# The state-space recurrence of an encoder layer: a predicated copy in place of mask products, and another order of a chunk's work on five engines

## The reference

```python
lower = idx[:, None] >= idx[None, :]
seg = a_cs[..., :, None] - a_cs[..., None, :]
decay = jnp.exp(jnp.where(lower, seg, -jnp.inf))
cb = jnp.einsum('bclgn,bcsgn->bgcls', cc, bc)
y_diag = jnp.einsum('bgcls,bgkcls,bcsgkp->bclgkp', cb, decay, xdt)
...
y = y_fwd + y_bwd + xs * d_skip.reshape(g, kh)[..., None]
y = (y.reshape(b, l, D_SSD) * jax.nn.silu(z)).astype(z.dtype)
```

## Time and profile before

| | us |
|---|---|
| median of 3 runs | 2933.29 |
| lowest, highest | 2931.94, 2934.85 |
| profiled execution, span | 2933.2 |
| PE busy | 2833.0 (97%) |
| DVE busy | 1997.4 (68%) |
| ACT busy | 1312.2 (45%) |
| POOL busy | 594.4 (20%) |

### The profile page before, as it was taken

One profiled execution on the slowest core, in us unless ns is written; L12 is line 12 of the kernel. 1 busy time (PEld: TensorE's weight loads), 2 busy tenths in 40 slices (PEclk: granted clock), 3 DMA queues, 4 the chain that ended last, 5 costly groups with the idle time before them and its releaser, 6 DMA issues.

```text
span 2933.2 us, 36790 instructions
## 1 busy us (share of the span) xinstructions
PE 2833.0 (97%) x12912; PEld 2244.0 (77%) x12912; DVE 1997.4 (68%) x3119; ACT 1312.2 (45%) x2578; POOL 594.4 (20%) x818
## 2 busy tenths in 40 slices
PE   7999999999999999999999999999999999999996
PEld 5878787667777878888778787876677788888885
DVE  3657755774788887775647567457757877777656
ACT  4224555455743333345543255553557433333443
POOL 4622222450014530000100222235400000000001
PEclk9999999999999999999999999999999999999998
DMA  7551232204535541243522422331246222214334
GB/s 223 140 147 56 63 106 91 95 27 154 181 129 191 177 164 58 87 155 114 201 94 74 125 63 73 117 130 28 68 141 199 79 80 76 68 58 156 96 115 140
DMA packets 143575, 332.75 MB, mean 113 GB/s; under 512 B 17745, under 2 KB 18417, under 8 KB 143392
## 3 DMA queue, kind: packets, MB, share of 16 engines
q1 hardware_dynamic: 106032, 200.42, 21.7%
q0 software_dynamic: 37360, 129.97, 13.4%
HBM read 264.49 MB, written 67.80 MB: 113 GB/s over the span
## 4 chain that ended last, share of the span: by engine, by line
PE 76%; DVE 11%; issue 5%; POOL 4%; ACT 3%; DMA 1%; SPq 0%; DVEq 0%; ACTq 0%; POOLq 0%
PE A L1076 4%; PE A L1078 4%; PE A L1077 4%; PE G L1076 4%; PE G L638 4%; PE G L1078 4%; PE G L1077 4%; PE G L640 4%; PE G L639 4%; PE A L1128 4%; PE A L1130 4%; PE A L1129 4%; PE G L668 3%; PE G L669 2%; PE G L670 2%
## 5 line engine op out<-in xcount | busy, mean ns | idle before, releaser
L1715 DVE TENSOR_TENSOR wlo<-raw,whi 128x512 fp32r<-128x512 f32 x630 | 437.3, 700 | 483.0 <-ACT whi L1204 480.9
L1204 ACT CAST whi<-raw 128x512 fp32r<-128x512 f32 x630 | 383.2, 619 | 448.6 <-PE A L1130 150.8
L638 PE MATMUL G<-arena_rounded,whi 128*128 128x512 f32 x800 | 330.6, 413 | 7.0 <-DVE wlo L1715 4.2
L640 PE MATMUL G<-arena_rounded,wlo 128*128 128x512 f32 x800 | 316.3, 395 | 0.0
L639 PE MATMUL G<-arena_rounded,whi 128*128 128x512 f32 x800 | 316.2, 395 | 0.0
L1076 PE MATMUL A<-arena_rounded,whi 128*128 128x512 f32 x560 | 222.0, 396 | 1.5 <-DVE wlo L1715 1.0
L1076 PE MATMUL G<-arena_rounded,whi 128*128 128x512 f32 x560 | 221.9, 396 | 0.8 <-DVE wlo L1715 0.7
L1078 PE MATMUL A<-arena_rounded,wlo 128*128 128x512 f32 x560 | 221.5, 396 | 0.0
L1078 PE MATMUL G<-arena_rounded,wlo 128*128 128x512 f32 x560 | 221.5, 395 | 0.0
L1077 PE MATMUL G<-arena_rounded,whi 128*128 128x512 f32 x560 | 221.5, 395 | 0.0
L1077 PE MATMUL A<-arena_rounded,whi 128*128 128x512 f32 x560 | 221.4, 395 | 0.0
(11 more groups left out here) (356 smaller groups left out, 6257.2 us busy)
## 6 DMA issues: line engine op xcount, KB each, us to landing
raw<-w_gu_tiles SPq DMA_DIRECT2D x184, 256.0 KB, 3.3
raw<-w_out_rows SPq DMA_DIRECT2D x144, 256.0 KB, 2.8
raw<-w_tok_tiles SPq DMA_DIRECT2D x96, 256.0 KB, 2.7
raw<-w_in_tiles SPq DMA_DIRECT2D x92, 256.0 KB, 2.8
raw<-sums_of_down SPq DMA_DIRECT2D x88, 256.0 KB, 2.6
raw<-w_down_rows SPq DMA_DIRECT2D x66, 256.0 KB, 2.7
f_by_chunk<-small POOLq DMA_DIRECT2D x24, 512.0 KB, 4.6
arena<-w_down_rows POOLq DMA_DIRECT2D x22, 512.0 KB, 7.4
```

What stands on the lines that cost most here:

```text
L638: nc.tensor.matmul(out, whi[:, u % SPLIT_SLOTS, w], hi, start=first, stop=False)
L640: return nc.tensor.matmul(out, wlo[:, u % SPLIT_SLOTS, w], hi, start=False, stop=last)
L1204: nc.scalar.copy(whi[:, u % SPLIT_SLOTS, w], weights_of(u)).then_inc(S["hi_split"], 1)
L1715: tt(wlo[:, u % SPLIT_SLOTS, w], weights_of(u), whi[:, u % SPLIT_SLOTS, w].bitcast(F), ALU.subtract).then_inc(S["lo_split"], 1)
```

## The change

The mask products go. PE's `exponents` has 4 matmuls per call instead of 8, and one semaphore at its end. A new DVE operation `pick(c, g)` copies the backward differences over the forward ones where the source token is later (`copy_predicated`, mask tile in SBUF, data and target in PSUM). ACT then takes a single exp into SBUF, and DVE multiplies that by `cb`, both from SBUF. The diagonal of the backward pass, which the copy leaves out, moves into the skip factor: `cb`'s diagonal is needed per token, so SP writes `rows` to DRAM and reads the diagonal back (256 elements of 4 bytes), and POOL makes a coefficient with two small operations (128x16) ahead of the wide one.

```diff
-    nc.tensor.matmul(to[:, n, :], ident_r[:, :], mask[:, :].unsqueeze(1).broadcast_to([P, 4, P]), start=True, stop=False)
-    m = nc.tensor.matmul(to[:, n, :], tmp_r[:, less:less + P], tmp_r[:, rhs:rhs + HALF], start=False, stop=True)
+    m = nc.tensor.matmul(to[:, n, :], tmp_r[:, less:less + P], tmp_r[:, rhs:rhs + HALF], start=True, stop=True)
...
+def pick(c, g):
+    dve.wait_ge(S["eb_done"], nth("eb_done", 2 * c + g + 1))
+    nc.vector.copy_predicated(by_heads(spans(ef_pair(c))), later[...].broadcast_to([P, GH, P]),
+                              by_heads(spans(eb_pair(c)))).then_inc(S["picked"], 1)
 def masses(c, g):
-    dve.wait_ge(S["eb_exp"], nth("eb_exp", 2 * c + g + 1))
-    after(tt(e, e, t(2 * g), ALU.add))
-    tt(t(2 * g + 1), e, cb(c, g), ALU.mult)
+    tt(t(2 * g + 1), t(2 * g), cb(c, g), ALU.mult)
...
-def gated(c):
-    after(tt(y_, y_, yb(c), ALU.add))
-    tt(arena[:, ZT + c, :], y_, arena[:, ZT + c, :], ALU.mult).then_inc(S["u_ready"], 1)
+def with_within(c):
+    tt(yb(c), spans(p2), yb(c), ALU.add).then_inc(S["y_read"], 1)
+def times_gate(c):
+    dve.wait_ge(S["y_read"], nth("y_read", c + 1))
+    tt(arena[:, ZT + c, :], yb(c), arena[:, ZT + c, :], ALU.mult).then_inc(S["u_ready"], 1)
```

The orders of a middle chunk after:

```diff
+PE:   incoming(c,SB) [waits for decays(c,1)], incoming(c,SF), exponents(c+1,0), within(c,0),
+      inner(c+1), exponents(c+1,1), state(c), within(c,1)
+DVE:  from_behind(c), from_ahead(c), pick(c+1,0), masses(c,1), times_gate(c-1), pick(c+1,1),
+      next_state(c), masses(c+1,0), with_within(c)
+POOL: add(from behind), scale SF, add(from ahead), scale x, with_skip(c+1) [waits for diag_in]
+SP:   load_exponents(c+1), save cb(c), wait, read its diagonal
```

More of the change, by code:

```diff
@@ L269, in encoder @@
         ones = sb("ones", [P, P])
-        ident_r, mask_f, mask_b = (ctx.enter_context(nc.sbuf_tensor(n, [P, P], R)) for n in ("ident_r", "mask_f", "mask_b"))
+        later = sb("later", [P, P])
+        dt_back = sb("dt_back", [P, TT, SH])
+        cb_diag = sb("cb_diag", [P, 2, GROUPS])
+        coef = sb("coef", [P, SH])
         last = ident[:, P - 1:P].broadcast_to([P, P])
@@ L609, in _ @@
                                  ).then_inc(S[f"z_back{i}"], 16)
[L610 to L612 removed]
+                for c in range(TT):
+                    if 1 <= c < TT - 1:
+                        sp.wait_ge(S["eb_done"], nth("eb_done", 2 * c))
+                        load_exponents(c + 1)
+                    sp.wait_ge(S["cb_out"], nth("cb_out", c + 1))
+                    sp.dma_start(cb_dram[c], rows[:, (c % 2) * 256:(c % 2 + 1) * 256]).then_inc(S["cb_saved"], 16)
+                    sp.wait_ge(S["cb_saved"], nth("cb_saved", 16 * (c + 1)))
+                    sp.wait_ge(S["yb_ready"], nth("yb_ready", max(0, c - 1)))
+                    sp.dma_start(cb_diag[:, c % 2, :], bass.AP(cb_dram.tensor, c * P * GROUPS * P, [[GROUPS * P + 1, P], [P, GROUPS]]), allow_slow_non_contiguous=True
+                                 ).then_inc(S["diag_in"], 16)
                 load(J_OUT, slice(4, None))
@@ L948, in _ @@
                 for c in range(TT):
-                    within(c, 0)
+                    if 0 < c < TT - 1:
+                        pe.wait_ge(S["ef_exp"], nth("ef_exp", 2 * c + 2))
+                        incoming(c, SB + c, p0, "yib_done")
                     if c:
@@ L2053, in _ @@
                 split_to(UNITS_TO[J_OUT] + 3)
+                pick(0, 0)
+                from_behind(0)
                 masses(0, 0)
-                from_behind(0)
-                masses(0, 1)
+                pick(0, 1)
                 for c in range(TT):
+                    if 0 < c < TT - 1:
+                        from_behind(c)
                     if c:
                         from_ahead(c)
-                    if c == 4:
+                    if c == 5:
                         roots(0)
                     if c < TT - 1:
+                        pick(c + 1, 0)
+                    masses(c, 1)
+                    if c:
+                        times_gate(c - 1)
+                    if c < TT - 1:
+                        pick(c + 1, 1)
+                        next_state(c)
                         masses(c + 1, 0)
@@ L2065, in _ @@
                         att_rest(0)
-                    gated(c)
-                    if c < TT - 1:
-                        next_state(c)
-                        masses(c + 1, 1)
-                    if c + 1 < TT - 1:
-                        from_behind(c + 1)
+                    with_within(c)
+                times_gate(TT - 1)
                 def mix_out(i):
```

153 lines of the change are left out of this document (79 added, 74 removed).

## The result

The changed kernel takes 2921.07 us, median of 6 runs (2915.53 to 2929.13), the kernel before 2934.58 in the same series (2931.94 to 2941.34): ratio 0.9959, 95% interval 0.9948 to 0.997. Two later series gave 2924.28 (0.997, 0.9958 to 0.9982) and 2925.73 (0.9967, 0.9954 to 0.998). By the ratios the change is worth 0.3 to 0.4%, some 9 to 12 us; the medians of the three series differ by 13.5, 6.8 and 8.0. Forecast was 2935, no change.

What follows compares the result with a forecast made beforehand. It took DVE and POOL shutting each other out to bound the changed chunk; fill 22.1 + 6 x 14.7 + drain 17.6 = 127.9 per sequence, +1.1 us on the 2933.2 span, put at 2935, range 2896 to 2958.

Steps and rivals of the forecast that it cites:

- The mechanism: Middle chunk of the recurrence: DVE operations with both inputs in SBUF and POOL shut each other out, taking back PE's gain.
- the sum of what cannot overlap: Middle chunk: POOL's 11.06 plus DVE's three blocked operations at 0.97 each make 14.0 us.
- The overlap rival: Middle chunk: masses and gate don't shut POOL out, DVE sets 11.7 to 12 us; whole kernel 2894 us; chance 0.16.
- the slow copy: DVE's pick: predicated copy takes 2.2 us, chunk 16.5, +15 per sequence, whole kernel 2963 us; chance 0.12.
- the clock's term: Middle chunk: PE's half-clock stretches after waits add 0.5 us per chunk (ends 0 and +1.5), giving 14.7.
- the laid-out chunk: Middle chunk scheduled instruction by instruction from incoming(c,SB): next incoming(SB) starts at 14.2 us, POOL never idle.
- Fill and drain: Recurrence's ends per sequence: fill before the six chunks falls from 29.6 to 22.1, drain after them rises from 13.0 to 17.6.
- worth less than 5.6: Fill: 16 mask products go, 6.4 us, of which some 5.6 were claimed to lie on PE's path.
- the clock stays full: Recurrence: no half-clock, chunk 14.0 to 14.2, fill 20.9, drain 15.4, whole kernel 2920 us; chance 0.16.
- Worth nothing by itself: ACT in a chunk: two exps of 1.03 us go, without gain except a shorter chain from exponents to masses.
- The diagonal at 0: DMA round trip of cb's diagonal, 5 to 8 us, ahead of with_skip: worth 0, at 8 us up to +0.3 a chunk.
- POOL's 11.06: POOL per middle chunk: three scalings and two additions, 10.46 us, plus two small operations at 0.3 each.

## Why the prediction was right and where it was wrong

*The mechanism was right.* The pick at 1.22; `masses` and `times_gate` at 1.2 to 3.4; POOL's operations at 2.8 to 3.3 beside them; POOL without idle; PE waiting 2 us ahead of incoming(SB) in every second chunk, 0.4 in the others; 13.9 to 14.2 between POOL's with_skips where the sum of what cannot overlap was 14.0. The overlap rival (a chunk near 11.9) and the slow copy fell with the first trace. The Trainium skill (SBUF — State Buffer, "Who interferes with whom") says that a DVE instruction with two SBUF inputs contends with a GpSimd one that reads SBUF. By that rule, the traces agree: `masses` takes 1.2 alone and up to 3.0 beside POOL.

*The step that failed is the clock's.* The prediction put 0.5 for half-clock stretches on every chunk, 14.7, where 13.86 was measured: 5 us too many a loop. Three of these are the clock's term; the rest is 0.2 by which the laid-out chunk (14.2) lay above the measured 13.99, and the shorter last chunk. The half-clock stretches came as forecast, 3.7 us for the incoming products behind a wait of 2.0, but beside a POOL that sets the pace: with_skip comes 13.86 after the one before where such a stretch begins (583.45 to 597.31), and 14.07 where none does (569.38 to 583.45). I had added a delay of PE to a chunk that I had just shown to be set by another engine. With `within` twice there are fewer of them, at no gain. They are not always free: 2.07 us once in the second profile, and in the drain, where PE is busy 17.8 of 18.6 us, the granted clock is 0.50 from 647 to 652.

*Fill and drain* took 24.2 and 18.6, not 22.1 and 17.6, which is 3 of the 5 us back. In the drain the clock has its part (0.72 against 0.87 before). In the fill it hasn't: 0.79 of 24.2 us and 0.83 of 29.6 are both 10 us at half clock. There the mask products were worth less than 5.6. The first four were on no path, as `incoming(0,SB)` waited for back_sum in both kernels and started at the same time (first line before, second after), and of the other twelve six, not all, stood at half clock, 0.43 apart, as the last two lines, of before, show: about 4 us in all (6 x 0.43 + 6 x 0.23).

```profile
536.99 3.78 PE L839 MATMUL G<-arena 128*128 128x512 f32 x4 [0.88 <-DVE arena L1959]
537.12 3.78 PE L850 MATMUL G<-arena 128*128 128x512 f32 x4 [1.60 <-DVE arena L1969]
549.26 0.63 PE L897 MATMUL G<-small_rounded 128*128 128x512 f32 x1
549.68 0.63 PE L896 MATMUL G<-mask_f,ident_r 128*128 128x512 f32 x1
```

Sum 125.9 against 127.9 forecast.

*A term was missing.* 2.05 and 1.2 us behind the two sequences' recurrences, where PE had waited for the gate and y_lo, were nobody's in the sum; the stretch that I read ended at turn_y(1).

*The bridge to the runs.* In the profiled execution, 2933.2 - 0.6 - 2.4 for the two recurrences and - 2.05 - 1.2 behind them make 2926.9, and the rest, + 0.9 between the sequences and - 0.4 at the end, the 2927.4 of the span. The median of the runs lies 8 us below the profiled one's 2929.13. So of the 14 us between forecast and median about 7.6 are accounted for by the profiled execution (4 in the recurrences, 3.3 behind them); the rest lies between its runs, outside the two loops as far as its three profiles show, and its cause stays open. In the runs of the changed kernel the granted clock is 0.986 to 0.991, before 0.990 to 0.993; in the changed kernel's, those at 0.991 took 2915.5 to 2919.6, those at 0.986 and 0.987 took 2924.4 to 2933.0. The profiled one, at 0.986, is the slowest of its six. The rival "the clock stays full", 2920, came nearest the median, by luck: its chunk (14.0) was right, but the clock didn't stay full, and its fill and drain (20.9, 15.4) were not met.

*The parts.* "Worth nothing by itself", the prediction says of the two ACT exps. ACT's time was no bound, but the chain through the exp was: the new order with mask products, two exps and an addition takes 16.64 a chunk, with as much PE work and one exp 14.58. And the copy in the old order shows that what the pick stands behind on DVE decides over 89 us. The diagonal at 0 is half right: its DMAs are never waited for in the changed kernel's loop (POOL once waited 4.7 for them where it had less work), its two small POOL operations cost the 0.5 a chunk (13.38 against 13.9) that the sum had as part of POOL's 11.06.

## What to carry to other kernels

When two engines shut each other out, add up the time of the one that is never idle and what the other holds it up, and then don't add a third engine's delays on top: a delay beside the bound costs nothing until it exceeds the slack, which an experiment that doubles that engine's work reads off. An operation put between a producer and its consumer on another engine (here the pick ahead of the exp) inherits the whole queue ahead of it, so its price is where it stands, not how long it runs. When a bound is lifted, look at the chain that was hidden at once: four single steps that each relieved POOL or took a meeting away gained nothing by the median, and two of them together did.

## What the runs showed of the hardware

- A predicated copy of 128x1024 fp32 from PSUM onto PSUM with a 32-bit mask in SBUF takes 1.22 us (1.205 to 1.230 in 28), as an operation with one PSUM operand; it neither waits for POOL nor holds it up (at 584.93, inside a POOL operation, it took 1.22, and POOL's next one 2.36).
- A DVE operation of 1024 columns with both inputs in SBUF holds POOL up by 0.9 to 1.0 us, for a scaling, an addition and even a small operation of 128x16, which goes from 0.22 to 1.20. A gate of only 64 columns took 1.93 beside a POOL scaling and 2.38 beside an addition, alone 0.22; it did not hold POOL's next addition up (2.36).
- Scaling 128x1024 per head costs POOL 1.90 in one operation, ACT 3.93 in sixteen of 64 columns (skip on ACT).
